# Seven raw chunks with their low parts in place, four high parts, and six chunks of the first expert loaded into idle memory during the router

## The chip, the core and the metric

The kernel runs on one core of one Trainium2 chip. The metric is the device time of that core in microseconds, the median of some runs of the whole program. The profile is of one execution.

## What is computed

The reference runs two blocks of two layers each on 256 tokens of width 1024. The first block is a hybrid layer (latent attention, short convolution, spatial gate, block attention). The second is a pooling and dilated attention mixer, with a dense feed-forward part in layer 0 and a mixture of experts in layer 1:

```python
def moe_swiglu(h, w_router, wg, wu, wd):
    xt = h.reshape(-1, D)
    logits = (xt @ w_router).astype(jnp.float32)
    top_v, top_i = lax.top_k(logits, TOP_K)          # 2 of 8
    gates = jax.nn.softmax(top_v, axis=-1)
    gate = jnp.sum(jax.nn.one_hot(top_i, N_EXPERTS) * gates[..., None], axis=1)
    y = jnp.zeros_like(xt)
    for e in range(N_EXPERTS):
        y = y + gate[:, e:e + 1] * swiglu(xt, wg[e], wu[e], wd[e])
```

Each expert has two matrices of 1024 x 3584 and one of 3584 x 1024, all float32.

## The kernel before

Every large weight streams through the core as "chunks" of 1 MB (128 partitions, KC = 4 rows of NC = 512 columns). For each chunk SyncE issues one transfer from HBM into a `raw` buffer (`sp_chunk`, L672), ScalarE rounds it into a "high part" `whi` (`act_hi` L921, in the experts `act_hi_moe` L929), VectorE subtracts to get the "low part" `wlo` (`dve_lo` L1296, in the experts `dve_lo_moe` L1304), and TensorE multiplies: low activations by high weights, high by low, and high by high. In the experts a heavy job has 128 token rows and 12 matrix products of 512 columns in a chunk (L2536 to L2538), a light job 64 rows and 8 products (L2551, L2552). In each halved step ScalarE and VectorE work on half a chunk per instruction.

Two rings of buffers set how far the engines run ahead. There are RAW = 6 raw buffers. SyncE may issue chunk n once `lo_ready` says that the low part of chunk n-6 is written. There are SPLIT = 3 pairs of high and low buffers. ScalarE may start chunk n once `split_used` says that TensorE has finished chunk n-3. Both numbers count over the whole program.

The work of every engine is an order written out by hand. Where the text of ScalarE or VectorE has `hi(i)` or `lo(i)` at position i, it works on chunk i + SPLIT; all other work of the engine (reading accumulators, activations, softmax) stands between these calls. Before the first layer both engines handle chunks 0 to SPLIT-1. In the first layer VectorE then does `lo(0)`, the sums of squares and the seed of the row scale (`squares`, `row_scale`), `lo(1)`, and the rotation angles (`angles`). GpSimd refines the row scale in `row_scale_pool` (L700 to L706) and raises `rs_ready`. ScalarE does `hi(0)`, `hi(1)`, the sine table (L1012), and only then reads the first projection out of PSUM (L970), which needs `rs_ready`. TensorE cannot take the fifth chunk before that.

The experts run as four pairs of jobs, 84 chunks (PER) each: 56 chunks of the two up matrices, with rows of 2 KB, and 28 of the down matrix, with rows of 4 KB. In the first pair (`FIRST_ORDER`) the heavy job is alone for LEAD = 12 chunks, whose weights are those of expert 0 and known before the router is done; the light job follows 12 chunks behind. From the light job on, SyncE needs the job table (`jobs_ready`). When a job's last down chunk is done, ScalarE copies the result (`y_read`), VectorE makes its low part (`y_lo`, L1974), TensorE carries it back to the tokens (`scatter`, L2511 and L2512), and VectorE adds it to `x` (L1963). In `pair` both engines do the chunk i + SPLIT first and the `y_read` or `y_lo` of position i after it. The last pair has nothing behind it, so the first SPLIT chunks of a stand-in (`moe_wg` of expert 0) are loaded and split there with no use; VectorE does the last two of them ahead of its final additions (L2040).

Of the kernel before, what the change touches and what calls it, by code (L numbers as in the profile page):

```python
# [19 lines left out]
F32 = mybir.dt.float32  # L20
# [107 lines left out]
RAW = 6  # L128
SPLIT = 3
KC = 4  # L130
# [117 lines left out]

LIGHT_PICK = 3
# [75 lines left out]
assert all(n % RAW == 0 for n in (len(HYBRID), AT_MIX0, AT_FFN, AT_MIX1, AT_MOE, PER))  # L325


def build(nc, A):

    ctx = ExitStack()  # L330
    with ctx:
# [55 lines left out]
        ahi2 = sb("ahi2", [PART, D_FFE], F32R, stack=moe)  # L387
        alo2 = sb("alo2", [PART, D_FFE], F32R, stack=moe)
        alT = sb("alT", [PART, D_FFE], F32R, stack=moe)
        act_h = sb("act_h", [PART, NC], stack=moe)  # L390
# [5 lines left out]
        yghi = sb("yghi", [PART, D], F32R, stack=moe)  # L396
        yglo = sb("yglo", [PART, D], F32R, stack=moe)
        pick = sb("pick", [PART, TILES, 2, PART], F32R, stack=moe)
        backT = sb("backT", [PART, 2, TILES, PART], F32R, stack=moe)
# [25 lines left out]
        moe.close()  # L425
        big, big2 = (gate_l[:, 128 * i:128 * i + 128].rearrange("p (t n) -> p t n", t=TILES) for i in range(2))
# [7 lines left out]
        raw_landed = [sem(f"raw_landed{i}") for i in range(RAW)]  # L434
        hi_ready = sem("hi_ready")
# [228 lines left out]
        def landed(c0, i, per=0, l=0):  # L664
            return 16 * (c0 // RAW + i // RAW + 1) + 16 * (per // RAW) * l


        def sp_chunk(sp, src, c0, i, chunk, per=0, l=0):
            if c0 + i >= RAW:

                sp.wait_ge(lo_ready, number(c0, i - RAW + 1, per, l))
            sp.dma_start(wide(raw[i % RAW]) if chunk.n == WIDE else raw[i % RAW][:, 0:chunk.k, 0:chunk.n],  # L672
                         src(chunk.k0 * PART, chunk.k * PART, chunk.n0, chunk.n)).then_inc(raw_landed[i % RAW], 16)
# [41 lines left out]
        def sync_program(sp):  # L715
# [31 lines left out]
            for i, step in enumerate(FIRST.steps):  # L747
                if i == LEAD + 1:
                    sp.wait_ge(jobs_ready, 1)
                    srcs[LIGHT_JOB] = expert(expert_at(1))  # L750
                sp_chunk(sp, srcs[step.b][step.chunk.which], AT_MOE, i, step.chunk)

            def pair(j):
                srcs = [expert(expert_at(2 * j + b)) for b in range(2)]
                for i, step in enumerate(PAIR.steps):
                    sp_chunk(sp, srcs[step.b][step.chunk.which], AT_MOE, i, step.chunk, PER, j)
# [10 lines left out]
            for i in range(SPLIT):  # L767
                sp_chunk(sp, rows(wg, 0), AT_MOE, i, PAIR.steps[i].chunk, PER, n_pairs)
# [143 lines left out]
        def act_hi(act, chunks, c0, i, per=0, l=0):  # L912

            n, k = split_shape(chunks[i % len(chunks)])
            act.wait_ge(raw_landed[i % RAW], landed(c0, i, per, l))
# [3 lines left out]
            for c in range(0, k, k // 2):  # L919

                nc.scalar.activation(whi[i % SPLIT][:, c:c + k // 2, 0:n], raw[i % RAW][:, c:c + k // 2, 0:n],  # L921
                                     ACT.Copy).then_inc(hi_ready, 1)

        def act_hi_moe(act, i, l):

            act.wait_ge(raw_landed[i % RAW], landed(AT_MOE, i, PER, l))
# [363 lines left out]
        def dve_lo(dve, chunks, c0, i, per=0, l=0):  # L1290

            n, k = split_shape(chunks[i % len(chunks)])
            for c in range(0, k, k // 2):

                dve.wait_ge(hi_ready, 2 * c0 + 2 * i + (2 if c else 1) + 2 * per * l)
                op = V.tensor_tensor(wlo[i % SPLIT][:, c:c + k // 2, 0:n], raw[i % RAW][:, c:c + k // 2, 0:n],  # L1296
                                     whi[i % SPLIT][:, c:c + k // 2, 0:n], ALU.subtract)
# [1433 lines left out]
```

## Time and profile before

| | us |
|---|---|
| median of 3 runs | 1587.7 |
| lowest and highest run | 1586.84, 1590.16 |
| span of the profiled execution | 1585.3 |
| TensorE matmul busy | 1519.5 (96%) |
| VectorE busy | 1293.3 (82%) |
| ScalarE busy | 1091.0 (69%) |
| read from HBM | 460.29 MB, 291 GB/s over the span |

The span reaches from the first to the last instruction. The page cuts it into 40 slices and gives in each the busy share of every engine, the granted TensorE clock and the rate of the DMA engines. The four pairs of experts fill about the last 920 us. Matmuls overlap each other, so that a full busy share of TensorE does not say that it could do no more.

### The profile page before, as it was taken

How to read it: one execution, taken by the hardware profiler on the slowest of the kernel's cores; microseconds unless marked ns; L12 is line 12 of the kernel's file. 1: busy time of each engine (PE TensorE's matmuls, PEld its weight loads, DVE VectorE, ACT ScalarE, POOL GpSimd, SP SyncE). 2: the span in 40 equal slices, each digit the busy share in tenths (PEclk: the TensorE clock that was granted, in tenths of full speed). 3: DMA queues.
4: the chain of work that ended last, by engine and by line, in shares of the span. 5: the costliest groups of instructions: out<-in, count | busy, mean ns of one | idle time of the engine just before them, and what ended most of it. 6: DMA issues, size and time to landing. Idle time of an engine off the chain costs nothing.

```text
span 1585.3 us, 20833 instructions
## 1 busy us (share of the span) xinstructions
PE 1519.5 (96%) x7379; PEld 1259.7 (79%) x7379; DVE 1293.3 (82%) x1595; ACT 1091.0 (69%) x1435; POOL 119.5 (8%) x242
## 2 busy tenths in 40 slices
PE   7999999999999999699999999999899999999995
PEld 5788788888888888588887788888788787788784
DVE  5686585566545556789999999999999999999998
ACT  3664565655434364278888788888788878788876
POOL 3433431101000010100000000000000000000000
PEclk9999999999999999699999999999999999999998
DMA  9645444535546554299999999999999999999995
GB/s 329 208 150 177 158 151 140 186 107 186 173 146 208 191 182 138 67 323 377 391 397 407 386 369 387 386 407 407 383 386 387 391 409 400 382 386 387 398 409 221
DMA packets 203364, 462.70 MB, mean 292 GB/s; under 512 B 7934, under 2 KB 12428, under 8 KB 203132
## 3 DMA queue, kind: packets, MB, share of 16 engines
q1 hardware_dynamic: 200304, 453.80, 78.5%
q0 software_dynamic: 1904, 5.38, 1.3%
q10 hardware_dynamic: 1052, 2.19, 0.4%
q8 instruction: 59, 0.97, 0.2%
q14 instruction: 45, 0.37, 0.1%
HBM read 460.29 MB, written 1.05 MB: 291 GB/s over the span
## 4 chain that ended last, share of the span: by engine, by line
PE 76%; DVE 10%; DMA 7%; issue 2%; DVEq 2%; ACT 2%; SPq 0%; ACTq 0%
PE ps L2080 8%; PE ps L2082 8%; PE ps L2081 8%; PE ps L2536 8%; PE ps L2538 7%; PE ps L2537 7%; PE ps L2551 7%; PE ps L2552 7%; DVE wlo_sb L1304 5%; DMA raw_sb<-moe_wu 4%; PE ps L2589 2%; DMA raw_sb<-w_in 2%; ACT whi_sb L929 1%; DMA raw_sb<-moe_wd 1%; PE ps L2498 1%
## 5 line engine op out<-in xcount | busy, mean ns | idle before, releaser
L1304 DVE TENSOR_TENSOR wlo_sb<-raw_sb,whi_sb 128x1024 fp32r<-128x1024 f32 x672 | 783.6, 1218 | 38.1 <-ACT whi_sb L929 35.8
L929 ACT ACTIVATE whi_sb<-raw_sb 128x1024 fp32r<-128x1024 f32 x672 | 667.2, 1051 | 156.5 <-PE ps L2538 102.5
L1296 DVE TENSOR_TENSOR wlo_sb<-raw_sb,whi_sb 128x1024 fp32r<-128x1024 f32 (+2 forms) x198 | 230.2, 1204 | 143.3 <-ACT whi_sb L921 142.3
L921 ACT ACTIVATE whi_sb<-raw_sb 128x1024 fp32r<-128x1024 f32 (+2 forms) x198 | 192.3, 1023 | 161.5 <-PE ps L2082 131.1
L2080 PE MATMUL ps<-whi_sb,xlo_sb 128*128 128x512 f32 (+2 forms) x544 | 213.2, 392 | 4.2 <-DVE xlo_sb L1343 4.2
L2081 PE MATMUL ps<-wlo_sb,xhi_sb 128*128 128x512 f32 (+2 forms) x544 | 209.0, 384 | 0.0
L2082 PE MATMUL ps<-whi_sb,xhi_sb 128*128 128x512 f32 (+2 forms) x544 | 208.9, 384 | 0.0
L2536 PE MATMUL ps<-whi_sb,xlo_sb 128*128 128x512 f32 x448 | 181.3, 405 | 4.5 <-DVE wlo_sb L1304 3.8
L2538 PE MATMUL ps<-whi_sb,xhi_sb 128*128 128x512 f32 x448 | 175.4, 391 | 0.0
L2551 PE MATMUL ps<-whi_sb,xhi_sb 128*128 128x512 f32 x448 | 175.2, 391 | 0.0
L2552 PE MATMUL ps<-wlo_sb,xhi_sb 128*128 128x512 f32 x448 | 174.6, 390 | 0.0
L2537 PE MATMUL ps<-wlo_sb,xhi_sb 128*128 128x512 f32 x448 | 174.5, 389 | 0.0
L2080 PEld LDWEIGHTS ps<-whi_sb,xlo_sb 128*128 128x128 f32 x544 | 103.3, 190 | 25.8 <-DVE wlo_sb L1296 4.4
L2082 PEld LDWEIGHTS ps<-whi_sb,xhi_sb 128*128 128x128 f32 x544 | 103.3, 190 | 19.6
L2081 PEld LDWEIGHTS ps<-wlo_sb,xhi_sb 128*128 128x128 f32 x544 | 103.5, 190 | 18.9 <-issue 0.5
L2536 PEld LDWEIGHTS ps<-whi_sb,xlo_sb 128*128 128x128 f32 x448 | 84.3, 188 | 20.4 <-DVE wlo_sb L1304 4.5
L2538 PEld LDWEIGHTS ps<-whi_sb,xhi_sb 128*128 128x128 f32 x448 | 84.1, 188 | 18.8
L2551 PEld LDWEIGHTS ps<-whi_sb,xhi_sb 128*128 128x128 f32 x448 | 84.1, 188 | 17.6 <-issue 0.2
L2552 PEld LDWEIGHTS ps<-wlo_sb,xhi_sb 128*128 128x128 f32 x448 | 84.1, 188 | 17.5
L2537 PEld LDWEIGHTS ps<-wlo_sb,xhi_sb 128*128 128x128 f32 x448 | 84.4, 188 | 15.8
L2551 PE MATMUL ps<-whi_sb,alT_sb 128*128 128x512 f32 x224 | 90.8, 405 | 3.9 <-DVE wlo_sb L1304 2.8
L2552 PE MATMUL ps<-wlo_sb,alT_sb 128*128 128x512 f32 x224 | 90.3, 403 | 0.0
(386 smaller groups left out, 2107.3 us busy)
## 6 DMA issues: line engine op xcount, KB each, us to landing
raw_sb<-moe_wg SPq DMA_DIRECT2D x115, 1024.0 KB, 9.7
raw_sb<-moe_wu SPq DMA_DIRECT2D x112, 1024.0 KB, 10.2
raw_sb<-moe_wd SPq DMA_DIRECT2D x112, 1024.0 KB, 10.8
raw_sb<-w_in SPq DMA_DIRECT2D x40, 1024.0 KB, 5.2
raw_sb<-w_out SPq DMA_DIRECT2D x16, 1024.0 KB, 5.0
raw_sb<-ffn_wg SPq DMA_DIRECT2D x10, 1024.0 KB, 5.1
raw_sb<-ffn_wu SPq DMA_DIRECT2D x10, 1024.0 KB, 5.1
raw_sb<-ffn_wd SPq DMA_DIRECT2D x10, 1024.0 KB, 5.1
```

The lines of the kernel that those rows point to most:

```text
L921: nc.scalar.activation(whi[i % SPLIT][:, c:c + k // 2, 0:n], raw[i % RAW][:, c:c + k // 2, 0:n], ACT.Copy).then_inc(hi_ready, 1)
L929: nc.scalar.activation(whi[i % SPLIT][:, c:c + KC // 2, :], raw[i % RAW][:, c:c + KC // 2, :], ACT.Copy).then_inc(hi_ready, 1)
L1296: op = V.tensor_tensor(wlo[i % SPLIT][:, c:c + k // 2, 0:n], raw[i % RAW][:, c:c + k // 2, 0:n], whi[i % SPLIT][:, c:c + k // 2, 0:n], ALU ...
L1304: op = V.tensor_tensor(wlo[i % SPLIT][:, c:c + KC // 2, :], raw[i % RAW][:, c:c + KC // 2, :], whi[i % SPLIT][:, c:c + KC // 2, :], ALU.su ...
L2080: mm(out, lo, whi[i % SPLIT][:, c, 0:chunk.n], start=first, stop=False)
L2081: mm(out, hi, wlo[i % SPLIT][:, c, 0:chunk.n], start=False, stop=False)
L2082: op = mm(out, hi, whi[i % SPLIT][:, c, 0:chunk.n], start=False, stop=last)
L2536: mm(o, lo, whi[i % SPLIT][:, w, :], start=first, stop=False)
L2537: mm(o, hi, wlo[i % SPLIT][:, w, :], start=False, stop=False)
L2538: op = mm(o, hi, whi[i % SPLIT][:, w, :], start=False, stop=last)
L2551: mm(o, both, whi[i % SPLIT][:, w, :], start=first, stop=False)
L2552: op = mm(o, both, wlo[i % SPLIT][:, w, :], start=False, stop=last)
```

## The change

There are seven raw buffers and four high buffers. A low part is written over the raw chunk that it was made of (the `wlo` tiles lie at the same addresses as the `raw` tiles), so a raw buffer comes free when TensorE has finished its chunk, seven back. In the experts each half-chunk pair of instructions on ScalarE and VectorE becomes one instruction of 128 x 2048. Chunks 7 to 12 of the first pair go to six other places: one spare buffer and five that lie in tiles of the expert stage which are not yet in use. These places take part in no ring: chunks 13 to 19 take the raw buffers of chunks 0 to 6, and chunk 20 takes that of chunk 13. Some tiles of the expert stage change places.

```diff
-RAW = 6
-SPLIT = 3
+RAW = 7
+SPLIT = 4
...
+AHEAD = tuple(range(RAW, RAW + 6))
...
+        over_raw = ExitStack()
+        wlo = [sb(f"wlo{i}", [PART, KC, NC], F32R, stack=over_raw) for i in range(RAW)]
+        wlo_spare = sb("wlo_spare", [PART, KC, NC], F32R, stack=over_raw)
+        over_raw.close()
         raw = [sb(f"raw{i}", [PART, KC, NC]) for i in range(RAW)]
+        raw_spare = sb("raw_spare", [PART, KC, NC])
         whi = [sb(f"whi{i}", [PART, KC, NC], F32R) for i in range(SPLIT)]
-        wlo = [sb(f"wlo{i}", [PART, KC, NC], F32R) for i in range(SPLIT)]
...
+        def ring_at(i, l):
+            return i if first(l) and i < AHEAD[0] else i - len(AHEAD)
...
+        def freed_moe(sp, i, l):
+            back = i - RAW
+            if first(l) and i >= AHEAD[0] and back < AHEAD[0] + len(AHEAD):
+                back -= len(AHEAD)
+            sp.wait_ge(split_used, number(AT_MOE, back + 1, PER, l))
...
+        def sp_ahead(sp, src, e, chunk):
+            if e == len(AHEAD) - 1:
+                sp.wait_ge(xn_lo, 1)
+            elif e:
+                sp.wait_ge(y_made, DEPTH + 2)
+            sp.dma_start(raw_ahead[e][:, 0:chunk.k, 0:chunk.n],
...
         def sp_chunk(sp, src, c0, i, chunk, per=0, l=0):
             if c0 + i >= RAW:
-                sp.wait_ge(lo_ready, number(c0, i - RAW + 1, per, l))
+                sp.wait_ge(split_used, number(c0, i - RAW + 1, per, l))
...
-            for i, step in enumerate(FIRST.steps):
-                if i == LEAD + 1:
-                    sp.wait_ge(jobs_ready, 1)
-                    srcs[LIGHT_JOB] = expert(expert_at(1))
-                sp_chunk(sp, srcs[step.b][step.chunk.which], AT_MOE, i, step.chunk)
+            for i in range(AHEAD[0]):
+                load_first(i)
+            for e, i in enumerate(AHEAD):
+                sp_ahead(sp, srcs[HEAVY_JOB][FIRST.steps[i].chunk.which], e, FIRST.steps[i].chunk)
+            sp.wait_ge(jobs_ready, 1)
+            srcs[LIGHT_JOB] = expert(expert_at(1))
+            for i in range(AHEAD[-1] + 1, PER):
+                load_first(i)
...
             act.wait_ge(split_used, number(AT_MOE, i - SPLIT + 1, PER, l))
-            for c in range(0, KC, KC // 2):
-                nc.scalar.activation(whi[i % SPLIT][:, c:c + KC // 2, :], raw[i % RAW][:, c:c + KC // 2, :],
-                                     ACT.Copy).then_inc(hi_ready, 1)
+            nc.scalar.activation(whi_of(AT_MOE, i)[:, :, :], moe_raw(i, l)[:, :, :], ACT.Copy).then_inc(hi_ready, 1)
...
-            for c in range(0, KC, KC // 2):
-                dve.wait_ge(hi_ready, 2 * AT_MOE + 2 * i + (2 if c else 1) + 2 * PER * l)
-                op = V.tensor_tensor(wlo[i % SPLIT][:, c:c + KC // 2, :], raw[i % RAW][:, c:c + KC // 2, :],
-                                     whi[i % SPLIT][:, c:c + KC // 2, :], ALU.subtract)
-            op.then_inc(lo_ready, 1)
+            dve.wait_ge(hi_ready, 2 * (AT_MOE + SPLIT) + i - SPLIT + 1 + PER * l)
+            V.tensor_tensor(moe_lo(i, l)[:, :, :], moe_raw(i, l)[:, :, :], whi_of(AT_MOE, i)[:, :, :],
+                            ALU.subtract).then_inc(lo_ready, 1)
```

## Rows read from the trace of the kernel before

**Rows 1.** Windows of the experts: us, busy PE, PEld, DVE, ACT, POOL, clock, DMA share, GB/s.

```profile
690.00:700.00 10.00, 10.00 (x55) 8.55 (x54) 8.70 (x15) 7.17 (x10) 0.00 (x0) 1.00 1.00 338
740.00:750.00 10.00, 10.00 (x51) 8.27 (x50) 10.00 (x11) 8.96 (x12) 0.00 (x0) 1.00 1.05 387
840.00:850.00 10.00, 10.00 (x49) 8.12 (x48) 9.60 (x11) 8.62 (x12) 0.00 (x0) 1.00 1.03 409
910.00:920.00 10.00, 8.74 (x47) 7.12 (x46) 9.91 (x10) 6.83 (x10) 0.00 (x0) 1.00 0.93 329
```

**Rows 2.** The page's costliest groups: the splitting of the experts' chunks.

```profile
L1304 DVE TENSOR_TENSOR wlo_sb<-raw_sb,whi_sb 128x1024 fp32r<-128x1024 f32 x672 | 783.6, 1218 | 38.1 <-ACT whi_sb L929 35.8
L929 ACT ACTIVATE whi_sb<-raw_sb 128x1024 fp32r<-128x1024 f32 x672 | 667.2, 1051 | 156.5 <-PE ps L2538 102.5
```

**Rows 3.** Timeline of SyncE's queue, experts' first chunks: start us, us, what.

```profile
644.30 29.56 SPq L672 DMA_DIRECT2D raw_sb<-moe_wg  x2
707.55 10.05 SPq L672 DMA_DIRECT2D raw_sb<-moe_wg  x4
719.45 8.01 SPq L672 DMA_DIRECT2D raw_sb<-moe_wu  x4
```

**Rows 4.** Timeline of ScalarE in the first job: in brackets idle time and what ended it.

```profile
670.02 2.01 ACT L929 ACTIVATE whi_sb<-raw_sb 128x1024 fp32r<-128x1024 f32 x2 [3.37 <-PE ps L2538]
710.87 2.01 ACT L929 ACTIVATE whi_sb<-raw_sb 128x1024 fp32r<-128x1024 f32 x2 [0.26 <-PE ps L2552]
```

**Rows 5.** Timelines of ScalarE, VectorE, GpSimd and TensorE, first 45 us.

```profile
32.97 2.01 ACT L921 ACTIVATE whi_sb<-raw_sb 128x1024 fp32r<-128x1024 f32 x2 [7.54 <-DMA raw_sb<-w_in]
40.30 1.25 ACT L970 ACTIVATE P_sb<-ps,rx_sb 128x512 f32<-128x512 f32 x2
24.51 2.36 DVE L1296 TENSOR_TENSOR wlo_sb<-raw_sb,whi_sb 128x1024 fp32r<-128x1024 f32 x2
34.06 2.36 DVE L1296 TENSOR_TENSOR wlo_sb<-raw_sb,whi_sb 128x1024 fp32r<-128x1024 f32 x2 [4.00 <-ACT whi_sb L921]
30.14 0.19 POOL L700 TENSOR_TENSOR rs_tmp_sb<-rx_sb 128x2 f32<-128x2 f32 x1 [11.20 <-DVE rx_sb L695]
33.61 0.19 POOL L702 TENSOR_TENSOR rs_tmp_sb<-rs_tmp_sb,ss_sb 128x2 f32<-128x2 f32 x1 [3.28 <-issue]
38.72 0.22 POOL L706 TENSOR_TENSOR rx_sb<-rx_sb,rs_tmp_sb 128x2 f32<-128x2 f32 x1
41.60 0.88 PE L2229 MATMUL ps<-con_sb,P_sb 128*128 128x128 f32 x6 [3.31 <-ACT P_sb L970]
```

**Rows 6.** Timeline of VectorE: one subtraction of 128x2048, and eight of 128x1024.

```profile
656.04 2.29 DVE L1829 TENSOR_TENSOR xnlo_sb<-xw_sb,xnhi_sb 128x2048 fp32r<-128x2048 f32 x1
714.69 9.39 DVE L1304 TENSOR_TENSOR wlo_sb<-raw_sb,whi_sb 128x1024 fp32r<-128x1024 f32 x8 [0.36 <-ACT whi_sb L929]
```

**Rows 7.** Three chunks issued up to 9.5 us: issue to landing; the last one's issue.

```profile
DMA to landing us min/median/max: 17.9/26.5/28.0
8.87 2.37 SPq L672 DMA_DIRECT2D raw_sb<-w_in  x1
```

**Rows 8.** The page's busy tenths of TensorE in 40 slices of the span.

```profile
PE   7999999999999999699999999999899999999995
```

**Rows 9.** Window behind that wait, columns as in rows 1.

```profile
42.00:44.00 2.00, 2.00 (x10) 1.63 (x9) 1.47 (x2) 2.00 (x4) 0.00 (x0) 0.59 1.05 385
```

**Rows 10.** Timelines of VectorE and TensorE where the second pair ends.

```profile
1112.95 1.28 DVE L1974 TENSOR_TENSOR yglo_sb<-ps,yghi_sb 128x512 fp32r<-128x512 f32 x2
1114.37 0.47 PE L2511 MATMUL ps<-yglo_sb,backT_sb 128*128 128x512 f32 x1 [1.37 <-DVE yglo_sb L1974]
```

**Rows 11.** Chunks issued between 1010 and 1020 us: issue to landing.

```profile
DMA to landing us min/median/max: 12.0/12.4/12.6
```

**Rows 12.** Timeline of VectorE at the end of the program.

```profile
1562.93 1.28 DVE L1974 TENSOR_TENSOR yglo_sb<-ps,yghi_sb 128x512 fp32r<-128x512 f32 x2
1570.37 4.62 DVE L1304 TENSOR_TENSOR wlo_sb<-raw_sb,whi_sb 128x1024 fp32r<-128x1024 f32 x4
```

More of the change, by code:

```diff
@@ L247 @@
 PAIR = plan_of(PAIR_ORDER, False)
+AHEAD = tuple(range(RAW, RAW + 6))
+assert all(FIRST_ORDER[i] == HEAVY_JOB for i in range(AHEAD[-1] + 1))
 LIGHT_PICK = 3
@@ L322, in head_scale_of @@
     return MLA_QK ** -0.5 if att < DEPTH and d < 2 else HD ** -0.5
-assert all(n % RAW == 0 for n in (len(HYBRID), AT_MIX0, AT_FFN, AT_MIX1, AT_MOE, PER))
+assert PER % RAW == 0 and PER % SPLIT == 0
 def build(nc, A):
@@ L434, in build @@
         raw_landed = [sem(f"raw_landed{i}") for i in range(RAW)]
+        ahead_landed = [sem(f"ahead_landed{e}") for e in range(len(AHEAD))]
         hi_ready = sem("hi_ready")
@@ L664, in landed, with raw_of, whi_of, wlo_of @@
         def landed(c0, i, per=0, l=0):
-            return 16 * (c0 // RAW + i // RAW + 1) + 16 * (per // RAW) * l
+            return 16 * ((c0 + i) // RAW + 1) + 16 * (per // RAW) * l
+        def raw_of(c0, i):
+            return raw[(c0 + i) % RAW]
+        def whi_of(c0, i):
+            return whi[(c0 + i) % SPLIT]
+        def wlo_of(c0, i):
+            return wlo[(c0 + i) % RAW]
+        def ring_at(i, l):
+            return i if first(l) and i < AHEAD[0] else i - len(AHEAD)
+        def moe_raw(i, l):
+            if first(l) and i in AHEAD:
+                return raw_ahead[AHEAD.index(i)]
+            return raw_of(AT_MOE, ring_at(i, l))
@@ L755, in pair @@
                 for i, step in enumerate(PAIR.steps):
-                    sp_chunk(sp, srcs[step.b][step.chunk.which], AT_MOE, i, step.chunk, PER, j)
+                    sp_chunk_moe(sp, srcs[step.b][step.chunk.which], i, step.chunk, j)
             for j in range(1, EXPERTS // 2):
@@ L767, in sync_program @@
             for i in range(SPLIT):
-                sp_chunk(sp, rows(wg, 0), AT_MOE, i, PAIR.steps[i].chunk, PER, n_pairs)
+                sp_chunk_moe(sp, rows(wg, 0), i, PAIR.steps[i].chunk, n_pairs)
             for n in range(2):
@@ L2079, in pe_chunk @@
                     first, last = chunk.first and c == 0, chunk.last and c == chunk.k - 1
-                    mm(out, lo, whi[i % SPLIT][:, c, 0:chunk.n], start=first, stop=False)
-                    mm(out, hi, wlo[i % SPLIT][:, c, 0:chunk.n], start=False, stop=False)
-                    op = mm(out, hi, whi[i % SPLIT][:, c, 0:chunk.n], start=False, stop=last)
+                    mm(out, lo, whi_of(c0, i)[:, c, 0:chunk.n], start=first, stop=False)
+                    mm(out, hi, wlo_of(c0, i)[:, c, 0:chunk.n], start=False, stop=False)
+                    op = mm(out, hi, whi_of(c0, i)[:, c, 0:chunk.n], start=False, stop=last)
             op.then_inc(split_used, 1)
@@ L2550, in light_step @@
                         w = c * (chunk.n // NC) + h
-                        mm(o, both, whi[i % SPLIT][:, w, :], start=first, stop=False)
-                        op = mm(o, both, wlo[i % SPLIT][:, w, :], start=False, stop=last)
+                        mm(o, both, whi_of(AT_MOE, i)[:, w, :], start=first, stop=False)
+                        op = mm(o, both, moe_lo(i, j)[:, w, :], start=False, stop=last)
                 op.then_inc(split_used, 1)
```

80 lines of the change are left out of this document (57 added, 23 removed).

## The prediction

> **What bounds the kernel now.** I read the windows first. In the experts' stage the DMA rate stands on one of two levels, whatever the engines do: 387 GB/s where the up matrices stream and 409 GB/s where the down matrices do [rows 1]. For a chunk of 1.0486 MB that is 2.71 us and 2.56 us, so a pair of 84 chunks (56 and 28) needs 223.5 us. Only before 720 us and around 910 us is the rate lower (338, 329). From about 720 us on, the end is therefore set by how many chunks have moved by then, by each time the DMA queue runs dry afterwards, and by what is left once the last chunk lands. The page's groups come second: the subtractions cost 783.6 us of VectorE and wait 38 us in all, and ScalarE waits longest for TensorE (102.5 us), not for data [rows 2]. So TensorE and VectorE are just behind the DMA: a delay of either can let the queue run dry. Third, before 720 us: SyncE's queue shows no issue between 644.7 and 673.5 us (the second start of the first row) [rows 3], and ScalarE's next chunk waits for TensorE each time [rows 4]: that stage is TensorE's. Fourth, the first 45 us, where TensorE stands still for 3.31 us until ScalarE has read the first projection [rows 5].
>
> All sums are made on the profiled span of 1585.3 us. The median of the runs is 1587.7 us, 2.4 us above it; I add that at the end. 0.2% (3.2 us) is about what a measurement of this kernel can tell from no change.
>
> **Part 1, the six chunks ahead.** Before, nine chunks are in when TensorE begins the experts; after, thirteen. Four chunks more are 4 x 2.71 = 10.8 us of transfers, the most that this part can give. But the six extra places are in no ring. Chunks 13 to 19 are issued as chunks 0 to 6 are finished, from 670.0 us on (there ScalarE takes up chunk 3, which waits for the end of chunk 0) [rows 4]. With seven steps from there, at the pace of 13 steps in 40.9 us (chunk 0 done at 670.0, chunk 13 at 710.9 [rows 4]), 3.15 us each, the last of them goes out at about 689 us. Chunk 20 needs the buffer of chunk 13, so it goes out at 710.9 us. Before, it went out at 707.6 us and chunk 24 at 719.4 us [rows 3]; after, chunk 24 waits for the end of chunk 17, about 720 us. The DMA engines are idle from about 695 to 711 us, and the four chunks' lead is gone before the DMA becomes the bound. What remains is chunk 20 late by 3.3 us and chunk 24 by some 0.6 us. I take **+1 us**, bounds 0 and +3.3. During the router the added transfers meet only idle queues (no issue for 29 us [rows 3]); I cost that at nothing.
>
> **Part 2, one instruction for a chunk.** Eight halves back to back take 9.39 us, so they start (9.39-1.22)/7 = 1.17 us apart, 2.33 us a chunk; one subtraction of 128x2048 takes 2.29 us [rows 6]. The halves overlap already, so VectorE gains 0.04 us a chunk, or 0.09 if the long ones overlap as the halves do, and that lies beside the DMA's 2.71 us. ScalarE has more room still. On the other side VectorE now starts after the whole high part and not after half of it, about one half (1.05 us [rows 2]) later. The fourth high buffer covers that. I take **0**, bounds -3 (the dip around 910 us cured) and +3.
>
> The Trainium skill ("VectorE: DVE Perf Modes", the section on the TRN2 errata for SBUF-source operations) says that such an instruction pays a fixed extra cost and that one large tile pays it once. Its formula of (N+151)/0.96 ns agrees with the 2.29 us row, and an estimate by it is 336 x 0.157 = 53 us of VectorE saved. By the starts of the halves in the row that cost is hidden, and the sum would be as above; by the rule it is the first rival below.
>
> **Part 3, the start.** This comes from SPLIT alone. `lo(0)` is chunk 4 now and not chunk 3, and on VectorE it stands ahead of the squares and the row scale; `hi(1)` is chunk 5 and stands ahead of the sine table and of the first projection's read (L970). Chunk 4 lands only at 32.97 us, since the constants and small weights share the queues [rows 5]. Its low part ends at 34.06+2.36 = 36.4 us. From the end of `lo(0)` to GpSimd's first step of the row scale it is 30.14-26.87 = 3.3 us now, so GpSimd starts at 39.7 us. Its chain ran from 30.14 to 38.94 us, 8.8 us, of which 3.28 us is a pause that the profile doesn't explain [rows 5]. With the pause `rs_ready` comes at 48.5 us, without it at 45.2 us. The other way: chunk 5 lands at 8.87+28.0 = 36.9 us [rows 7], is rounded by 39.0, its low part is made from 39.7 to 42.0, and the angles take what they take now, 40.3-36.4 = 3.9 us: 45.9 us. So L970 starts at 45.9 to 48.5 us and not at 40.3 us: +5.6 to +8.2 us. I take **+8.2**, since it is the same chain of instructions under the same DMA load. From 41.6 us on TensorE is busy in all slices up to the router [rows 8], so nothing takes this back. A longer stand may also lengthen the time at the low clock (0.59 granted behind a stand of 3.3 us [rows 9]); up to +1.
>
> In the other layers the same shift by one chunk costs nothing: `split_used` is asked for the same count at the same place, and a chunk there has three TensorE steps to land.
>
> **Part 4, the ends of the pairs.** `y_lo` at position i comes behind chunk i+4 now, so one more chunk is taken up on both engines before a result is passed to `scatter`. In the second pair VectorE makes that low part at 1112.95 us and TensorE takes it at 1114.37 after standing 1.37 us [rows 10]. One whole chunk more is 2.3 us of VectorE and about 1.3 us for its landing and high part: TensorE is 3.6 us late at each of three ends. A queue that is full (12.4 us from issue to landing before such an end [rows 11]) absorbs most; the ring that frees only after TensorE gives it less room. Nothing lost is one bound, 3.6 us and a fall of the clock (2 us) at each the other. I take a third, 3 x 1.3 = **+4**, bounds 0 and +16.
>
> **Part 5, the end of the program.** Four stand-in chunks follow instead of three. The last heavy result (VectorE at 1562.93) now stands behind the first of them, the same 3.6 us: it lands 2.71 us behind the last real chunk, and VectorE's subtraction takes 2.29 us. The two last stand-ins ahead of the final additions stay two (4.62 us at 1570.37) [rows 12]. Nothing hides it, since the chain there runs through VectorE. **+3.7**, bounds +2.3 and +4.7.
>
> **Sum:** 1 + 0 + 8.2 + 4 + 3.7 = 16.9 us: a span of 1602.2 us, and with the 2.4 us outside it **1604.6 us**.
>
> **The rivals.**
> First, faster: the merge pays. If VectorE sets the pace of the experts, its halves cost what each is listed with, 2 x 1.218-2.29 = 0.146 us a chunk, and 336 chunks give 49 us [rows 2, 6]; with the other parts 1604.6-49 = 1555.6 us. For it: VectorE is 10.00 busy of 10 at 740 us. Against it: the level of 387 GB/s in the same row [rows 1], which this can't lift. It decides only if that level is the engines' pace and not the DMA's. The rule of the skill above would give this. 0.03.
> Second, faster: the lead holds and the start is free. It decides if chunk 13 were done before chunk 19 lands: -10.8+3.7 = -7, 1580.6 us. Against it stands the pace of 3.15 us. 0.05.
> Third, nothing: start and ends are absorbed, 1588 us. 0.05.
> Fourth, the start is absorbed (chunk 4 lands sooner, or the row scale isn't last), the rest holds: 1604.6-8.2 = 1596.4 us. 0.20.
> Fifth, slower still: at each pair's end TensorE stands over 5 us, its clock falls to 1.2 GHz as it did behind the 3.3 us stand [rows 9], and the queue runs dry: Part 4 is 16 and not 4, 1616.6 us. For it: the rate fell to 329 GB/s behind the first pair [rows 1]. 0.15.
> The forecast itself has 0.52.
>
> **How the numbers follow.** Forecast, fourth and fifth rival hold 0.87. The range reaches from 1593 us (the fourth with its small bounds) to 1615 us, which leaves out about 0.2. Slower by over 0.2%: 0.87; within: 0.05; faster: 0.08.
>
> **What would show it.** L970 begins at 46 to 49 us and not at 40.3. SyncE's queue shows chunk 20 at its old time plus the start's shift plus 3 us, behind a gap of some 20 us. The levels of 387 and 409 GB/s stay. One low part more stands ahead of the last heavy result. A first projection read at 40 us, or a level above 387 GB/s, would make the prediction wrong.

## The result, and the profile after

The changed kernel takes 1642.7 us (median, 1639.9 to 1648.8) where the kernel before takes 1588.9 us (1586.8 to 1590.3) on the same chip: a ratio of 1.0342 (95% interval 1.0326 to 1.0358), 53.8 us slower. The forecast was 1604.6 us with a range of 1593 to 1615. The direction was right, and the size was off by 38 us, outside the range and beyond even the slowest rival (1616.6).

The profiled execution of after is the slowest of its four (1648.8 us). Its span is 1647.0 us, 61.7 us more than that of before. Its page, section 2 and the groups that split the experts' chunks, which answer to [rows 2]:

```profile
PEclk9899999999999998899999999999999999999997
...
GB/s 332 151 146 178 169 138 151 159 122 179 178 189 168 213 129 221 245 186 387 396 402 362 340 386 384 395 371 372 317 384 370 387 370 344 344 361 386 370 387 193
...
L1395 DVE TENSOR_TENSOR wlo_sb<-raw_sb,whi_sb 128x2048 fp32r<-128x2048 f32 x330 | 751.7, 2289 | 103.3 <-ACT whi_sb L1022 99.6
L1022 ACT ACTIVATE whi_sb<-raw_sb 128x2048 fp32r<-128x2048 f32 x330 | 630.5, 1917 | 217.9 <-PE ps L2628 80.1
```

From slice 19 on, the rates of 387 and 396 to 402 GB/s are still there, but between them stand slices of 317 to 372. The idle time of VectorE ahead of these subtractions rose from 38.1 to 103.3 us, of which ScalarE ended 35.8 and 99.6 us. Most of the experts' time lies in one window, 740 to 1540 us. First before, then after (columns as in [rows 1]; the last three are the granted clock, DMA share and GB/s):

```profile
740.00:1540.00 800.00, 779.21 (x3691) 641.05 (x3690) 770.19 (x776) 664.15 (x785) 0.00 (x0) 1.00 1.04 393
```

```profile
740.00:1540.00 800.00, 748.56 (x3471) 610.41 (x3470) 713.49 (x442) 610.87 (x461) 0.00 (x0) 0.98 1.00 372
```

The transfers run at 372 GB/s and not at 393. To move what before moved in these 800 us, after needs 800 x (393/372 - 1) = 45 us more. That is the larger part of the loss, and it lies in the middle of the experts, for which the sum had the 4 us of Part 4.

**Where the rate is lost.** The second pair's end, which answers to [rows 10], on the timeline of after:

```profile
1135.87 1.06 ACT L1296 ACTIVATE yghi_sb<-ps 128x512 fp32r<-128x512 f32 x2
1135.99 2.29 DVE L1395 TENSOR_TENSOR wlo_sb<-raw_sb,whi_sb 128x2048 fp32r<-128x2048 f32 x1 [0.42 <-ACT whi_sb L1022]
...
1138.20 1.28 DVE L2064 TENSOR_TENSOR yglo_sb<-ps,yghi_sb 128x512 fp32r<-128x512 f32 x2
...
1139.63 0.77 PE L2601 MATMUL ps<-yglo_sb,backT_sb 128*128 128x512 f32 x1 [4.36 <-DVE yglo_sb L2064]
```

TensorE's last matmul before it ended at 1135.3 us. The low part of y starts at 1138.20, behind a whole low part of a chunk (1135.99), and TensorE stands for 4.36 us where it had stood for 1.37. Windows of 5 us over what follows:

```profile
1135.00:1140.00 5.00, 0.64 (x3) 0.40 (x2) 4.58 (x5) 4.26 (x5) 0.00 (x0) 0.80 1.05 387
1140.00:1145.00 5.00, 5.00 (x13) 3.84 (x13) 3.88 (x2) 1.38 (x1) 0.00 (x0) 0.51 1.01 373
1145.00:1150.00 5.00, 5.00 (x24) 4.08 (x23) 1.98 (x1) 3.93 (x4) 0.00 (x0) 1.00 0.62 209
1150.00:1155.00 5.00, 2.32 (x11) 1.61 (x10) 4.91 (x6) 3.16 (x3) 0.00 (x0) 1.00 1.03 366
1155.00:1160.00 5.00, 5.00 (x17) 3.92 (x16) 3.48 (x2) 0.23 (x1) 0.00 (x0) 0.66 0.22 85
1160.00:1165.00 5.00, 5.00 (x24) 4.13 (x23) 3.28 (x2) 4.68 (x4) 0.00 (x0) 1.00 0.83 274
```

The clock falls to 0.80 and 0.51 of its higher level (0.51 is nearly all at the 1.2 GHz level), TensorE is busy for only 2.32 of 5 us some 15 us later, and the DMA rate falls to 209, 85 and 274 GB/s, each time some 5 us behind TensorE. The same happens away from the pairs' ends. In the up phase, at the transposes of one block of h (the product of the two up projections, which VectorE makes), and the windows behind it:

```profile
1239.21 0.66 PE L2725 MATMUL ps<-con_sb,act_h_sb 128*128 128x128 f32 x4 [2.14 <-DVE act_h_sb L2074]
```

```profile
1240.00:1245.00 5.00, 5.00 (x17) 3.94 (x16) 4.24 (x3) 3.32 (x4) 0.00 (x0) 0.66 1.00 365
1245.00:1250.00 5.00, 5.00 (x28) 4.25 (x27) 3.75 (x2) 3.26 (x3) 0.00 (x0) 1.00 0.94 316
```

The low clock adds to the stand: on the timeline eight matmuls between 1240.40 and 1243.76 us start some 0.42 us apart where they start 0.23 us apart before and after. By these starts it costs another 1.5 us (an estimate), so TensorE is 3.6 us late and not 2.14.

Over the stage (740 to 1600 us) the waits of this kind, by engine and line: total us, times, longest. After:

```profile
PEld ps L2725 <- DVE act_h_sb L2074: 38.4, 24, 2.7
...
PE ps L2725 <- DVE act_h_sb L2074: 28.3, 24, 2.2
...
PE ps L2601 <- DVE yglo_sb L2064: 16.3, 5, 4.4
```

And before:

```profile
PEld ps L2635 <- DVE act_h_sb L1984: 12.4, 24, 1.5
...
PE ps L2511 <- DVE yglo_sb L1974: 8.1, 5, 2.0
...
PE ps L2635 <- DVE act_h_sb L1984: 4.9, 5, 1.1
```

TensorE's matmuls stood 4.9 us for the product of h and now stand 28.3 us, 24 times and not 5. (The PEld rows are the weight loads of the same transposes, so the two rows of a kernel are not to be added. The rows of the y parts don't cover the same ends: before, this window holds the end of the program too, after, it doesn't. Over the whole span they are 8.1 and 21.7 us.)

**How long the queue was.** From issue to landing, the chunks issued from 1000 to 1040 us, mid in a pair. Before:

```profile
DMA to landing us min/median/max: 11.4/12.2/13.1
```

After:

```profile
DMA to landing us min/median/max: 7.7/8.6/9.5
```

A chunk on idle queues takes 5.1 us (5.2 on the page of before), as the page's row for w_in has it:

```profile
raw_sb<-w_in SPq DMA_DIRECT2D x40, 1024.0 KB, 5.1
```

So each chunk before had some 7 us of other chunks' transfers ahead of it, and after it has 3.5 us. As an estimate, that is the time for which TensorE may be late before the DMA engines have nothing to do. A stand of 4.4 us with a low clock behind it is more than 3.5 us, and one of 2.14 us reaches it with what the clock adds.

### The profile page after: what moved, and what is told of

It reads as the page before. It is cut to its first block, busy times and chain, and to the rows that moved or that the text cites. A ratio compares the mean times of both kernels' runs of the same rounds, so it can differ in the third digit from the quotient of the medians.

```text
span 1647.0 us, 20081 instructions
## 1 busy us (share of the span) xinstructions
PE 1539.1 (93%) x7379; PEld 1269.5 (77%) x7379; DVE 1280.2 (78%) x1261; ACT 1073.1 (65%) x1101; POOL 116.6 (7%) x242
## 3 DMA queue, kind: packets, MB, share of 16 engines
HBM read 461.34 MB, written 1.05 MB: 281 GB/s over the span
## 4 chain that ended last, share of the span: by engine, by line
PE 67%; DVE 10%; DMA 9%; issue 6%; ACT 4%; DVEq 2%; POOL 0%; POOLq 0%; SPq 0%; ACTq 0%
DMA raw_sb<-moe_wg 8%; PE ps L2170 8%; PE ps L2172 8%; PE ps L2171 8%; PE ps L2626 6%; PE ps L2628 6%; PE ps L2627 6%; DVE wlo_sb L1395 5%; PE ps L2641 5%; PE ps L2642 5%; ACT whi_sb L1022 4%; PE ps L2679 2%; PE ps L2588 1%; PE ps L2725 1%; DVE act_h_sb L2074 1%
## 5 line engine op out<-in xcount | busy, mean ns | idle before, releaser
L1395 DVE TENSOR_TENSOR wlo_sb<-raw_sb,whi_sb 128x2048 fp32r<-128x2048 f32 x330 | 751.7, 2289 | 103.3 <-ACT whi_sb L1022 99.6
L1022 ACT ACTIVATE whi_sb<-raw_sb 128x2048 fp32r<-128x2048 f32 x330 | 630.5, 1917 | 217.9 <-PE ps L2628 80.1
L2642 PE MATMUL ps<-wlo_sb,xhi_sb 128*128 128x512 f32 x448 | 175.7, 392 | 0.0
L2627 PE MATMUL ps<-wlo_sb,xhi_sb 128*128 128x512 f32 x424 | 166.2, 392 | 0.0
L2172 PEld LDWEIGHTS ps<-whi_sb,xhi_sb 128*128 128x128 f32 x544 | 103.3, 190 | 19.6
L2626 PE MATMUL ps<-whi_sb,alo_sb 128*128 128x512 f32 x224 | 90.1, 402 | 0.5 <-DVE wlo_sb L1395 0.2
```

What stands on the lines that cost most here:

```text
L1022: nc.scalar.activation(whi_of(AT_MOE, i)[:, :, :], moe_raw(i, l)[:, :, :], ACT.Copy).then_inc(hi_ready, 1)
L1395: V.tensor_tensor(moe_lo(i, l)[:, :, :], moe_raw(i, l)[:, :, :], whi_of(AT_MOE, i)[:, :, :], ALU.subtract).then_inc(lo_ready, 1)
L2172: op = mm(out, hi, whi_of(c0, i)[:, c, 0:chunk.n], start=False, stop=last)
L2626: mm(o, lo, whi_of(AT_MOE, i)[:, w, :], start=first, stop=False)
L2627: mm(o, hi, moe_lo(i, j)[:, w, :], start=False, stop=False)
L2642: op = mm(o, both, moe_lo(i, j)[:, w, :], start=False, stop=last)
```

## The experiments

The theory: in the experts each engine's other work (silu, the h product, the parts of y) now stands behind the split of chunk i+4 and not of i+3, so TensorE gets its operands one chunk later. Only 7 - 4 = 3 ring chunks are left for transfers, so each lateness reaches the DMA queue. The rivals: one instruction per chunk delays the low parts; the ring, whose chunks TensorE frees, is too short whatever the order; the loads ahead do harm.

All runs in one table: us over the kernel before, each against its own runs of before on the same chip (1587.8 to 1589.1 us), with the ratio's 95% interval. "High" and "raw" are the numbers of buffers, "left" is the number of ring chunks beyond the split ones, "split" the chunk that a step at position i splits, "instr" the instructions for a chunk.

```
run                  high raw left split  instr  us over before   interval of the ratio
changed kernel         4   7   3   i+4    one      +53.8          1.0326 to 1.0358
a_look3                4   7   4   i+3    one       +3.1          1.0011 to 1.0030
a_split3               3   7   4   i+3    one      +22.8          1.0127 to 1.0161
a_halves               4   7   3   i+4    two      +39.1          1.0224 to 1.0258
b_merge (before +)     3   6   6   i+3    one      +20.8          1.0111 to 1.0145
a_look3_halves         4   7   4   i+3    two       +0.1          0.9993 to 1.0010
a_look3_noahead        4   7   4   i+3    one       +4.6          1.0017 to 1.0039
a_noahead              4   7   3   i+4    one      +53.3          1.0309 to 1.0350
a_split3_halves        3   7   4   i+3    two       +7.4          1.0035 to 1.0070
a_yfirst               4   7   3   i+4*   one      +40.6          1.0243 to 1.0278
a_look3_raw6           4   6   3   i+3    one      +24.7          1.0137 to 1.0171
b_used (before +)      3   6   3   i+3    two      +28.3          1.0166 to 1.0200
a_raw6                 4   6   2   i+4    one     +123.8          1.0755 to 1.0791
a_hfirst               4   7   3   i+4*   one      +41.3          1.0235 to 1.0274
a_allfirst             4   7   4   i+4*   one      +12.5          1.0063 to 1.0100
a_look2_halves         4   7   5   i+2    two      +35.5          1.0205 to 1.0242
```

(* some or all of the other work moved ahead of the split. With all of it ahead, as in a_allfirst, the order is that of i+3, and 4 chunks are left.)

**a_look3**, the position alone:

```diff
 SPLIT = 4
+LOOK = 3
...
-                    act_hi_moe(act, i + SPLIT, j)
+                    act_hi_moe(act, i + LOOK, j)
...
-                        dve_lo_moe(dve, i + SPLIT, j)
+                        dve_lo_moe(dve, i + LOOK, j)
```

(and so in every other place that names i + SPLIT, in the first loop of each engine, in the stand-ins at the end and in the count that VectorE waits for)

> The changed kernel with its buffers as they are (7 raw, 4 high, six ahead, one instruction per chunk), but every step of ScalarE and VectorE that split chunk i+4 now splits chunk i+3, as before the change. Theory (the position: in the experts the silu, the h product, the y parts stand behind one more chunk, TensorE waits for them, so the raw chunks that it frees come late): the start term (+5.6) and the stands at the pair ends go, TensorE's waits for VectorE at the h transposes fall from 28.3 + 38.4 us to about the 4.9 + 12.4 of before, time about 1595 (1588 to 1605). Rival ring (a ring of 7 whose chunks TensorE frees is too short whatever the order): only the start goes, about 1635. Rival merge: the same, 1635.

Measured 1592.2 us: 50.7 of the 53.8 us are gone, with every buffer and the single instruction kept. The waits fell less than expected: TensorE's for the h product are 13.9 us (15 times) and those of its weight loads 20.8 us. Taking the split back by one chunk does two things at once. The other work no longer stands behind one more chunk, and one more ring chunk is left for transfers (4 and not 3). a_look3_raw6 below takes the two apart.

**a_split3**, three high buffers (`SPLIT = 3`, nothing else):

> The changed kernel with 3 high buffers in place of 4 (so the split of chunk i+3 in each step, and ScalarE waits for TensorE to be done with chunk i before it). Theory position: as a_look3 within 10 us, about 1600; if ScalarE's wait for TensorE costs by itself, it is slower than a_look3. Rival ring: about 1635. Rival merge (one instruction with only three high buffers starts VectorE later with no cover): over 1640.

1612.0 us, between, and outside the 10 us of the theory. The same position with one high buffer fewer is 20 us slower than a_look3.

**a_halves**, the two instructions per chunk back:

```diff
-            nc.scalar.activation(whi_of(AT_MOE, i)[:, :, :], moe_raw(i, l)[:, :, :], ACT.Copy).then_inc(hi_ready, 1)
+            for c in range(0, KC, KC // 2):
+                nc.scalar.activation(whi_of(AT_MOE, i)[:, c:c + KC // 2, :], moe_raw(i, l)[:, c:c + KC // 2, :],
+                                     ACT.Copy).then_inc(hi_ready, 1)
```

(and the like on VectorE, which waits for each half)

> The changed kernel with each expert chunk split by two instructions of 128x1024 on ScalarE and two on VectorE again, all else as changed. Theory position: 1642 within 8 us, most likely a little faster since VectorE starts one half part (1 us) earlier. Rival merge: 1595 to 1600, the loss goes but for the start. Rival ring: 1642.

1628.3 us: 14.7 us of the loss are gone, more than the 8 us of the theory and far less than the rival's loss. The merge is not free, but it isn't the main cause.

**b_merge**, the kernel before with the opposite of that diff:

> The kernel before with one 128x2048 instruction per expert chunk on ScalarE and VectorE, nothing else. Theory position: 1588 within 5 us. Rival merge: 1620 to 1640, since each chunk's low part comes about 1 us later after its high part and there is no fourth buffer as cover. My recorded estimate for the merge was 0 (-3 to +3) with the fourth buffer as cover; without it I expect at most +5.

1610.0 us, 20.8 us slower: my theory gave it 5 at most. The waits of b_merge from 740 to 1600 us, which for the kernel before were 86.3 us (77 times) and 28.1 us (65 times):

```profile
ACT whi_sb L928 <- PE ps L2534: 138.7, 112, 5.3
DVE wlo_sb L1301 <- ACT whi_sb L928: 69.3, 100, 3.2
```

ScalarE waits for TensorE to free a high buffer. With three buffers that is a closed loop, worked out here from durations and not tested by itself: the end of chunk i, the high part of i+3 (1.92 us), its low part (2.29 us), TensorE on i+3, while TensorE has only i+1 and i+2 to do. One heavy and one light chunk are 12 and 8 matmuls that follow each other every 0.235 us in the trace of after (1133.47, 1133.70), 4.7 us in all, against 4.2 us for the two parts, and the h product (0.68 us), the silu or another small step stands between them in some turns. In halves VectorE starts one half (1.05 us) sooner.

**a_look3_halves**, both undone, the buffers and the six chunks kept:

> The changed kernel with chunk i+3 split in each step (4 high buffers kept) and each expert chunk split by two instructions again; left of the change: the fourth high buffer, low parts over the raw chunks, 7 raw, six ahead. Measured so far: the split position alone gave 1592.2, the halves alone 1628.3. Theory (two causes, one loop: the latency from landing to low part, times how far the other work stands behind): the halves are worth little where a spare high buffer covers them, 1588 (1583 to 1592). Rival (merge costs its 14 us wherever it stands): 1578.

1588.6 us, the same as before. So the merge costs 20.8 us in the kernel before, 15.4 us with the new ring and three high buffers (a_split3 less a_split3_halves), 14.7 us in the changed kernel and 3.0 us at i+3 with a spare high buffer. A fourth buffer does cover it, but only where it is spare: if the split of i+4 takes it at once, it covers nothing.

**a_split3_halves**, what the ring alone does (`SPLIT = 3` and halves):

> The changed kernel with 3 high buffers, the position of before (i+3) and two instructions per expert chunk: what is left of the change is the ring alone (7 raw with the low part written over, freed by TensorE, and the six ahead). Theory: the ring is no cause, 1588 to 1594. Rival ring: 1610 or more, since a chunk's buffer is held until TensorE is done with it.

1595.9 us, 7.4 us slower: more than the upper end that the theory gave for "no cause", far below the rival.

**a_look3_noahead** and **a_noahead**, the loads ahead:

```diff
-AHEAD = tuple(range(RAW, RAW + 6))
+AHEAD = ()
```

(with the first job's loads in one loop again)

> a_look3 without the six chunks in idle memory (the first job's chunks go round the ring of 7). Theory (the six chunks are loaded earlier but the next ones wait for a ring chunk that TensorE frees, so they are worth only what seven in the ring lack against the lead of before): 1598 (1592 to 1604), since without them the ring of 7 holds one chunk fewer than the 6 + 3 of before at the router. Rival: they are worth nothing, 1592; or their whole transfer time, 6 x 2.6 = 16 us, 1608.

> The changed kernel without the six chunks in idle memory, all else as changed. Theory: the six chunks did no harm; without them 1645 to 1655. Rival (the loads ahead and the idle queue after them cause the loss): 1600.

1593.1 and 1641.8 us: within a microsecond or two of their partners (1592.2 and 1642.7). The six chunks bring nothing and cost nothing, at either position. My theories had 1598 and 1645 to 1655; the first time is that of the rival "worth nothing", the second lies below the range. SyncE's queue shows why. Chunks 13 to 23 in a_look3 (chunk 20 begins the last row):

```profile
670.43 5.58 SPq L741 DMA_DIRECT2D raw_sb<-moe_wg  x3
...
710.44 7.79 SPq L741 DMA_DIRECT2D raw_sb<-moe_wg  x4
```

Chunk 20 without any chunk ahead:

```profile
710.33 7.77 SPq L738 DMA_DIRECT2D raw_sb<-moe_wg  x4
```

710.44 and 710.33 us: in both kernels chunk 20 waits until TensorE has finished chunk 13, however early chunk 13 was loaded. This is Part 1 of the prediction, confirmed.

**a_yfirst**, the pair ends alone:

```diff
-                    y_first = i == PER - 1 and not isinstance(j, int)
+                    y_first = i in plan.y_out
...
+                    if i in plan.y_out:
+                        y_lo(j, plan.y_out[i])
                     if not last_of_loop:
                         dve_lo_moe(dve, i + SPLIT, j)
```

> The changed kernel with one step moved: in the step that ends a job (four pairs, two jobs each) ScalarE reads y, and VectorE makes its low part, ahead of the split of chunk i+4 instead of behind it. This prices the pair ends alone. By my recorded term (1.3 us at each of three ends) 1639. By the stands and the clock that the trace of the changed kernel shows at the second end (TensorE stands 4.36 and 2.68 us, clock down to 0.51, DMA down to 85 GB/s) about 10 us at each end: 1612 to 1620. Rival (the h products of the up phase are the loss, not the ends): 1640.

(and the old place of `y_lo` behind it removed)

1628.9 us, 13.2 us better and less than the stands had suggested. Part of that is the last result of the program, which moved too: from the landing of the last real chunk to the end it is 30.0 us here and 33.0 in the changed kernel. That leaves some 10 us for the three pair ends, where the term was 4.

**a_hfirst**, the heavy job's up phase alone: silu and the copy of h ahead of `act_hi_moe`, the product of h at value chunk i+1 ahead of `dve_lo_moe(i + SPLIT)`, and the low part of h too.

> The changed kernel with the up phase of the heavy job put in its old place: ScalarE's silu and its copy of the transposed h ahead of the split of chunk i+4, VectorE's h product ahead of the low part of chunk i+3, its low part of h ahead of that of i+4. Theory (seven blocks of h in each pair, each a chunk late, starve the queue): together with the pair ends (1628.9 alone, 13.8 us) this makes the 44 us that are not the start, so 1612 (1605 to 1620). Rival (after the pair ends what is left is the short queue, whatever the order): 1640.

1629.0 us, 12.5 us better, not the 30 that I wanted to find there.

**a_allfirst**, all of it, in the experts only:

> The changed kernel with all other work of a step on ScalarE and VectorE ahead of the split of chunk i+4 in the experts, only there. 7 raw, 4 high, six ahead and one instruction stay, and so does the late start (+6). Theory (the fourth high buffer is harmless and the place of the other work is the whole loss of the experts): a_look3 plus the start, 1598 (1594 to 1602). Rival: 1615 or more, then something else of the changed kernel costs the rest.

1600.2 us, in the range given. In the experts this is the order of a_look3, written the other way, so it repeats that run there and leaves the start at i+4. Order alone, with the buffers, the merge and the late start as changed, brings 41.3 us. The two parts tried singly add up to 25.7 us; the other 15.6 us are the light job's steps or what the parts bring only together, and no run tells these apart. The second pair's end in it, where the changed kernel had 4.36:

```profile
1122.61 0.47 PE L2598 MATMUL ps<-yglo_sb,backT_sb 128*128 128x512 f32 x1 [1.69 <-DVE yglo_sb L2063]
```

Its window and its queue (issue to landing, from 1000 to 1040 us), beside 372 GB/s and 8.6 us:

```profile
740.00:1540.00 800.00, 777.17 (x3679) 638.29 (x3678) 753.07 (x476) 646.43 (x486) 0.00 (x0) 1.00 1.04 391
```

```profile
DMA to landing us min/median/max: 10.0/11.3/12.3
```

**a_look3_raw6**, **b_used** and **a_raw6**, the length of the ring:

```diff
-RAW = 7
+RAW = 6
```

(a_look3_raw6 and a_raw6) and, in the kernel before, for all stages:

```diff
-                sp.wait_ge(lo_ready, number(c0, i - RAW + 1, per, l))
+                sp.wait_ge(split_used, number(c0, i - RAW + 1, per, l))
```

> a_look3 with 6 raw chunks in place of 7: beyond the chunks that are split ahead of TensorE only 3 remain for transfers, as in the changed kernel (7 less 4). Theory (the changed kernel loses because the other work of ScalarE and VectorE stands a chunk later): about 1600, at most 1605. Rival (the loss is the short queue: 3 chunks beyond the split ones don't keep the DMA engines busy): 1635 or more.

> The kernel before with one wait changed: a raw chunk is loaded again when TensorE is done with it, not when its low part is made. 6 raw, 3 high, 3 low, halves: 3 chunks beyond the split ones, where before had 6. The price of the short queue by itself. Theory position: 1595 (1590 to 1602). Rival queue: 1625 or more.

> The changed kernel with 6 raw chunks in place of 7: 2 chunks beyond the split ones. If the queue is part of the loss, one chunk less makes it clearly worse, 1670 to 1700; if it is not, 1645. Both theories allow some loss here; it gives the slope of time against the length of the ring at the late position.

1612.9, 1616.6 and 1712.1 us. Here the theory missed: I had held the short queue for harmless where the order is the old one. The rivals of the first two (1635 and 1625 or more) were not reached either, and a_raw6 is beyond the 1700 that I gave. At i+3 the step from 4 chunks left to 3 costs 21.6 us; at i+4 the step from 3 to 2 costs 70 us. In a_look3_raw6 the order is right and the queue as short as in the changed kernel, and so is its rate below 391 GB/s:

```profile
740.00:1540.00 800.00, 764.07 (x3601) 620.38 (x3600) 739.26 (x466) 633.10 (x477) 0.00 (x0) 1.00 1.03 383
```

```profile
DMA to landing us min/median/max: 7.6/8.6/9.6
```

In a_look3_raw6 TensorE's clock stays at 1.00 in this window, and its longest stands for the h product and for y are 1.2 and 1.9 us, below the 3.5 us. A stand is not needed. Where the down matrices stream, the small products of L2589 (they gather the next jobs' rows) stand between the chunks for some 20 us, heavy chunks start 6.5 us apart (1293.9, 1300.4, 1307.0 us), and two chunks in 6.5 us are 320 GB/s. First a_look3_raw6, then the same stretch of the kernel before, with the same 6.5 us:

```profile
1290.00:1320.00 30.00, 30.00 (x146) 24.90 (x145) 26.21 (x21) 21.20 (x16) 0.00 (x0) 1.00 0.94 344
```

```profile
1270.00:1300.00 30.00, 30.00 (x150) 25.09 (x149) 27.70 (x36) 23.47 (x29) 0.00 (x0) 1.00 1.02 409
```

TensorE is busy throughout in both. Only the longer queue of before carries the transfers over it at 409 GB/s; a_look3, with one ring chunk more than a_look3_raw6, moves 386 GB/s there (1280 to 1310 us).

So the loss has one mechanism with two halves: TensorE is behind, by a stand, a low clock or more work, and the queue is too short to cover it. As an estimate from the runs, 21.6 of the 50.7 us that a_look3 wins are the ring chunk and 29.1 us the position, with the late start and the end among the 29.1. The fourth case, split at i+4 with 4 chunks left (8 raw buffers), was not run, so whether the two add up is open. Nor does a run tell what the clock adds by itself: in the changed kernel it is 0.98 over 800 us where it was 1.00, some 16 us at most by these rows, but it falls because TensorE stands.

The table's column "left" goes with the time for most rows: 3 left is +25 to +54, 4 left with the old order +0 to +23, and within that the merge and the spare buffer decide. b_merge (6 left, +20.8) and the next run (5 left) show that it is not the only thing.

**a_look2_halves**, one chunk earlier still:

> a_look3_halves (1588.6) with the split of chunk i+2 in each step in place of i+3: the other work stands one chunk earlier still, and 5 of 7 ring chunks are left for transfers. Theory (at i+3 the experts run at the rate of the transfers, 387 to 409 GB/s, and earlier brings nothing): 1588 to 1595. Rival (each chunk earlier brings some more): 1575. If the two light chunks of TensorE don't cover the time of the high and low part: over 1610.

1623.2 us, the third of these cases: 5 chunks left don't help if the parts are made too late. In it ScalarE stands ahead of its splits until TensorE has the gate ready, 53.6 us where it is 2.9 us in a_look3_halves (line, total us, times, longest):

```profile
ACT act_h_sb L1315 <- PE ps L2633: 53.6, 22, 2.6
```

## Why the prediction was off

Of the 61.7 us between the two spans, 6.9 had come up when TensorE finished the experts' chunk 0 (676.9 us where it was 670.0), 47.6 between there and the landing of the last real chunk, and 7.2 behind it. The sum had 5 us for the middle (Parts 1, 2 and 4). Three of its steps failed there: the shift by one chunk has no term in the experts' up phase, "The fourth high buffer covers that" in Part 2, and "A queue that is full absorbs most" in Part 4.

**Part 1 (+1): right.** The loads ahead are worth nothing within the noise. The queue shows chunks 13 to 19 out by 695.5 us, a gap of 23 us, and chunk 20 at 718.87:

```profile
676.88 5.59 SPq L740 DMA_DIRECT2D raw_sb<-moe_wg  x3
684.67 10.79 SPq L740 DMA_DIRECT2D raw_sb<-moe_wu  x4
718.87 7.78 SPq L740 DMA_DIRECT2D raw_sb<-moe_wg  x4
```

Chunk 20 is 11.3 us behind its time in [rows 3]: the start's 5.6 us, the 3.3 us of the sum and some 2 us more. The run without the loads ahead gives the same time within 1 us.

**Part 2 (0): wrong, 14.7 us.** The working with the starts of halves held in its result: VectorE's busy time fell by 0.05 us a chunk (751.7/330 against 783.6/336). The gain it gave is too small where merged low parts follow each other without a pause: two take 4.48 us in the last row of Part 5 below, so they start 2.20 us apart against 2.33 us for two halves, a gain of 0.13 us and not 0.09. In the experts VectorE often waits for ScalarE first, and gets less. The step that failed is the sentence "The fourth high buffer covers that". With SPLIT at 4, the split of chunk i+4 takes the fourth buffer, so the later low part goes through to TensorE and to the ring. Only with the buffer left spare the cost is 3.0 us. The first rival (the merge pays, 49 us) is refuted here: VectorE doesn't set the pace, and in four pairs of kernels one instruction was 3.0 to 20.8 us slower than two. By the Trainium skill ("VectorE: DVE Perf Modes", the section on the TRN2 errata for SBUF-source operations) one large tile pays the fixed cost of an instruction only once, 0.157 us a chunk by the prediction's estimate; the 0.13 us of the trace come near to that, but the kernel had no use for it.

**Part 3 (+8.2, bounds 5.6 to 8.2): the mechanism right, 5.6 us measured, the lower bound.** ScalarE at the start of the program, which answers to [rows 5]:

```profile
32.83 2.01 ACT L1015 ACTIVATE whi_sb<-raw_sb 128x1024 fp32r<-128x1024 f32 x2 [7.95 <-DMA raw_sb<-w_in]
36.97 2.01 ACT L1015 ACTIVATE whi_sb<-raw_sb 128x1024 fp32r<-128x1024 f32 x2 [2.12 <-DMA raw_sb<-w_in]
...
45.90 1.27 ACT L1062 ACTIVATE P_sb<-ps,rx_sb 128x512 f32<-128x512 f32 x2 [0.20 <-POOL rx_sb L792]
```

Chunk 4 lands at 32.83 us and the projection's read starts at 45.90, 5.6 us later than the 40.30 of before. The pause of 3.28 us in GpSimd's chain, which I had kept, is 1.40 us on the timeline of after, and the chain takes 6.3 us (39.55 to 45.81) and not 8.8. "It is the same chain" was the wrong reason for the upper end.

**"In the other layers the same shift costs nothing": true of those layers, and the gap of the sum.** Chunk 13 is issued at 676.88 us, when TensorE has finished chunk 0; before, it had done so at 670.0 us [rows 4]. That is 6.9 us later with the start's 5.6 in it, so the layers between added only 1.3 us. But the experts' up phase, with the same shift, has no term in the sum at all. I looked for the shift at the pair ends only, where the rows already showed a stand. The h product has one in the trace of before as well (24 waits of the weight loads, 12.4 us), and I didn't ask what one more chunk would do to it. a_allfirst less a_yfirst shows 28.1 us beside the pair ends.

**Part 4 (+4, bounds 0 to 16): mis-sized, some 10 us measured (13.2 less the 3.0 of the program's end).** The size of the stand was about right, 3.0 us more than before where I had 3.6. What failed is "A queue that is full (12.4 us from issue to landing before such an end) absorbs most". That is the queue of the kernel before, whose 6 ring chunks were all free for transfers. With 3 left, the queue of after is 8.6 us long and absorbs some 3.5 us. I had written that the ring "gives it less room" and didn't work it out. The fifth rival had this mechanism, but for the pair ends alone, at 16 us and for stands over 5 us; the longest in the experts is 4.4 us, and the clock and the DMA rate fell all the same.

**Part 5 (+3.7, bounds 2.3 to 4.7): the delay right, the end mis-sized, 7.2 us measured.** The last real chunk, the last heavy y and TensorE behind it, before (VectorE's y is in [rows 12]):

```profile
1559.56 2.01 ACT L929 ACTIVATE whi_sb<-raw_sb 128x1024 fp32r<-128x1024 f32 x2 [0.54 <-DMA raw_sb<-moe_wd]
1560.65 2.36 DVE L1304 TENSOR_TENSOR wlo_sb<-raw_sb,whi_sb 128x1024 fp32r<-128x1024 f32 x2 [0.20 <-ACT whi_sb L929]
...
1564.27 0.50 PE L2511 MATMUL ps<-yglo_sb,backT_sb 128*128 128x512 f32 x1 [1.62 <-DVE yglo_sb L1974]
```

After, with a window behind TensorE's stand and the last stand-ins:

```profile
1614.03 1.92 ACT L1022 ACTIVATE whi_sb<-raw_sb 128x2048 fp32r<-128x2048 f32 x1 [0.58 <-DMA raw_sb<-moe_wd]
1615.98 2.29 DVE L1395 TENSOR_TENSOR wlo_sb<-raw_sb,whi_sb 128x2048 fp32r<-128x2048 f32 x1 [0.20 <-ACT whi_sb L1022]
...
1622.04 1.28 DVE L2064 TENSOR_TENSOR yglo_sb<-ps,yghi_sb 128x512 fp32r<-128x512 f32 x2
...
1623.38 0.80 PE L2601 MATMUL ps<-yglo_sb,backT_sb 128*128 128x512 f32 x1 [5.41 <-DVE yglo_sb L2064]
...
1623.00:1630.00 7.00, 6.62 (x16) 5.01 (x16) 4.87 (x4) 1.92 (x1) 0.00 (x0) 0.53 0.13 49
...
1632.12 4.48 DVE L1395 TENSOR_TENSOR wlo_sb<-raw_sb,whi_sb 128x2048 fp32r<-128x2048 f32 x2
```

From the start of the last real chunk's high part to the end of the span it is 33.0 us where it was 25.7. From that chunk's low part to y it is 6.1 us where it was 2.3: 3.8 us, the delay that the sum had. From y to the end it is 25.0 us where it was 22.4, another 2.6 us: TensorE stood 5.41 us, and the clock behind that was 0.53 for 7 us where it was 1.00 before. The remaining 0.9 us is the merge, since the low part starts behind a whole high part. The sum had no term for these two.

a_allfirst over a_look3, 9.4 us, is not the sum of Parts 3 and 5: the start is in it, but the last y stands ahead of the stand-in there, and its end is only 1.9 us longer than that of a_look3.

The levels of 387 and 409 GB/s stayed, as said, but I took "the level stays" for "the rate stays". The end is set by the share of time at the level, and that share is bought by the length of the queue.

No version here beats the kernel before: the best, a_look3_halves, is level with it, at the same 387 to 409 GB/s.

## What to carry to other kernels

Where one constant sets both the number of buffers and the position of the work that is ordered by hand, raising it delays all that stands behind that work by one step; price each such step, and give the new buffer a position of its own first. The slack of a transfer-bound stage is the time from issue to landing less that on an idle queue; work it out for the new ring before you say that the queue absorbs a stand, and hold stretches against it in which the consumer merely has more work. And a merge that costs an engine nothing can still lengthen the path to the first use: here it was nearly free (3.0 us) only where a buffer stood spare.

## What the runs showed of the hardware

From 1000 to 1040 us the DMA engines move 387 GB/s in after with 8.6 us from issue to landing, and 389 GB/s in before with 12.2 us. The shorter queue costs nothing there; it costs where TensorE falls behind, by a stand or by more work (344 GB/s against 409 in a stretch in which TensorE is busy throughout in both). One ring chunk less costs 21.6 us at the early position and 70 us at the late one. A stand of TensorE of 2.14 us was followed by a window at 0.66 of the clock, one of 4.36 us by windows at 0.80 and 0.51, and one of 5.41 us by 7 us at 0.53. Behind the first two the DMA rate fell within 10 us. The prediction's fifth rival had tied the fall to stands over 5 us. Subtractions of 128x2048 that follow each other without a pause start 2.20 us apart though each is listed with 2.29, and pairs of 128x1024 take 2.33 us.
